# Attention heads in pairs: two heads share one PSUM accumulation, one product for the early keys of both, outputs taken out once per pair

## What is computed

```python
q = rope_tail(rms_norm(q, g_q_mla), cos, sin)      # MLA heads, 96 wide, values 64 wide
k = rope_tail(rms_norm(k, g_k_mla), cos, sin)
o_mla = blocked_causal_attention(pad_front(q), pad_front(k), pad_front(v_mla), MLA_QK ** -0.5)[:, PAD:]
...
o_fox = blocked_causal_attention(pad_front(qf), pad_front(kf), pad_front(vf), FOX_DIM ** -0.5, cum_log_f)[:, PAD:]
return jnp.concatenate([o_mla, o_fox], axis=-1) @ w_out
```

## Time and profile before

| | |
|---|---|
| median of 3 runs | 1344.78 us (1343.36 to 1344.78) |
| the profiled execution's own time | 1342.53 us |
| its span, first to last instruction | 1340.7 us |
| PE busy over the span | 1312.6 us (98%) |
| DVE, ACT, POOL busy | 969.4, 742.1, 362.3 us |
| granted PE clock, mean | 0.998 |

### The profile page before, as it was taken

How to read it: one execution, slowest core, us unless ns; L and a number is a source line. 1 busy time by engine, 2 the same in 40 slices (tenths; PEclk the granted TensorE clock), 3 DMA queues, 4 the chain that set the end, 5 groups by cost and what they waited for, 6 DMA issues and landing times. The chain is left out here.

```text
span 1340.7 us, 28848 instructions
## 1 busy us (share of the span) xinstructions
PE 1312.6 (98%) x10790; PEld 1289.3 (96%) x10790; DVE 969.4 (72%) x1462; ACT 742.1 (55%) x1198; POOL 362.3 (27%) x388
## 2 busy tenths in 40 slices
PE   9998999999999999999999999999999989999997
PEld 8887899999999999999999999999999989999997
DVE  6868877755487777555665669998559897999844
ACT  5456654444444554444546557666457986766642
POOL 4532133310011233100636214333102101433310
PEclk9999999999999999999999999999999999999999
DMA  9430245555554455555525545554554445555451
GB/s 314 161 114 1 82 172 188 188 192 186 184 182 167 157 198 185 208 180 177 208 103 187 191 158 201 183 184 159 189 212 164 175 165 189 194 186 185 159 194 55
DMA packets 35372, 230.53 MB, mean 172 GB/s; under 512 B 4062, under 2 KB 5214, under 8 KB 11910
## 3 DMA queue, kind: packets, MB, share of 16 engines
q1 hardware_dynamic: 34228, 226.99, 48.2%
q10 hardware_dynamic: 1058, 2.38, 0.5%
HBM read 228.17 MB, written 1.05 MB: 171 GB/s over the span
## 5 line engine op out<-in xcount | busy, mean ns | idle before, releaser
L382 DVE TENSOR_TENSOR wlo<-raw,whi 128x1024 fp32r<-128x1024 f32 (+1 forms) x446 | 526.1, 1182 | 89.7 <-ACT whi L376 87.6
L417 PE MATMUL ps<-xhi,whi 128*128 128x256 f32 (+2 forms) x2048 | 579.7, 283 | 3.8 <-DVE wlo L382 2.6
L418 PE MATMUL ps<-xlo,whi 128*128 128x256 f32 (+2 forms) x2048 | 577.9, 282 | 0.0
L419 PE MATMUL ps<-xhi,wlo 128*128 128x256 f32 (+2 forms) x2048 | 576.7, 282 | 0.0
L376 ACT ACTIVATE whi<-raw 128x1024 fp32r<-128x1024 f32 (+2 forms) x444 | 447.1, 1010 | 148.1 <-PE ps L419 138.4
L417 PEld LDWEIGHTS ps<-xhi,whi 128*128 128x128 f32 x2048 | 386.5, 189 | 8.8 <-issue 4.6
L419 PEld LDWEIGHTS ps<-xhi,wlo 128*128 128x128 f32 x2048 | 387.2, 189 | 0.0
L418 PEld LDWEIGHTS ps<-xlo,whi 128*128 128x128 f32 x2048 | 384.7, 188 | 0.3
L417 PE MATMUL ps<-hhi,whi 128*128 128x256 f32 (+1 forms) x1184 | 334.2, 282 | 4.5 <-DVE hlo L1706 3.6
L419 PE MATMUL ps<-hhi,wlo 128*128 128x256 f32 (+1 forms) x1184 | 333.2, 281 | 0.0
L418 PE MATMUL ps<-hlo,whi 128*128 128x256 f32 (+1 forms) x1184 | 333.0, 281 | 0.0
(11 more groups left out here) (303 smaller groups left out, 1274.6 us busy)
## 6 DMA issues: line engine op xcount, KB each, us to landing
raw<-w SPq DMA_DIRECT2D x182, 1024.0 KB, 4.8
raw<-w SPq DMA_DIRECT2D x40, 768.0 KB, 4.2
raw<-w SPq DMA_DIRECT2D x4, 512.0 KB, 5.3
h<-x_fm ACTq DMA_DIRECT2D x4, 272.0 KB, 5.6
out_fm<-h SPq DMA_DIRECT2D x8, 128.0 KB, 2.0
ws<-ws_src ACTq DMA_DIRECT2D x1, 512.0 KB, 3.6
bs<-bs_rows ACTq DMA_DIRECT2D x1, 512.0 KB, 5.0
consts<-constants SPq DMA_DIRECT2D x1, 508.0 KB, 10.3
```

The source lines that it names most:

```text
L382: nc.vector.tensor_tensor(wlo[:, w, 0:n], raw[:, slot, col:col + n], whi[:, w, 0:n].bitcast(F32), ALU.subtract).then_inc(wlo_done, 3 if fr ...
L417: nc.tensor.matmul(o, hi, xh, start=start, stop=False)
L418: nc.tensor.matmul(o, hi, xl, start=False, stop=False)
L419: mm = nc.tensor.matmul(o, lo, xh, start=False, stop=stop)
```

## The change

Two heads with neighbouring numbers (0 and 1, 2 and 3, ...) form a pair `k` and share one output bank (4 or 5, by `k`). The values are laid out anew: `v_main` holds for each pair three slots of 64 columns, the first head's values, zeros, the second head's values. A head's stationary operand is two neighbouring slots, so the other head's rows get zeros added, and both heads accumulate into all 128 rows of one bank. `v_early` holds the 16 early keys of the first head in rows 0 to 15 (columns 0 to 63) and those of the second in rows 32 to 47 (columns 64 to 127), and one product does both at the end of the second head's `values`. The first block's product now has 258 columns, since `prob_t` gets two zero columns ahead.

The narrow transposes of both heads are made in the `turn` of the second head (`second(j)`), into bank 6 always: first two that put the second head in rows 32 to 47, then two for the first head in rows 0 to 15. One ACT copy of 48 rows takes both to `prob_0`. `high` and `low` run once per pair, on all 128 rows. The probabilities get 4 buffers instead of 3, the d items a place of their own. d1 moves one place back in the list, to item 11, so its `turn` is at step 13. The constant `four` lies in a part of `extra`, and POOL clears two more small areas and one of 1024 columns. The copies of the 16 early keys' values by ACT are now two of 256 columns instead of one of 512, in each of the two attentions.

```diff
-        items = ([("d", 0)] + [("h", i) for i in range(HEADS)] + [("h", HEADS), ("d", 1)]
-                 + [("h", HEADS + i) for i in range(1, HEADS)])
+        items = ([("d", 0)] + [("h", i) for i in range(HEADS + 2)] + [("d", 1)]
+                 + [("h", HEADS + i) for i in range(2, HEADS)])
...
+        def second(j):
+            return items[j][0] == "h" and items[j][1] % 2 == 1
+        def early_turned(j):
+            return sum(items[x][0] == "d" or second(x) for x in range(j))
...
             def turn(j):
...
-                elif j <= LAST_SHARED:
-                    pe.wait_ge(pt0_done, j)
-                else:
-                    turn_bank = 6 + (j - LAST_SHARED) % 2
-                    pe.wait_ge(pt0_done, j - 1)
-                    pe.wait_ge(k_out, 2 * HEADS)
+                elif j < 6 or kind == "d" or second(j):
+                    pe.wait_ge(pt0_done, early_turned(j))
...
-                for x, a in enumerate((A, B)):
-                    nc.tensor.transpose(ps[0:META, turn_bank, x * P:(x + 1) * P], pr[:, a:a + META], ident)
+                if second(j):
+                    at = i % 4 * NPR
+                    for x, a in enumerate((A, B)):
+                        nc.tensor.transpose(ps[0:3 * META, 6, x * P:(x + 1) * P],
+                                            wide[:, at + a - 2 * META:at + a + META], ident)
+                    for x, a in enumerate((A, B)):
+                        nc.tensor.transpose(ps[0:META, 6, x * P:(x + 1) * P],
+                                            wide[:, at - NPR + a:at - NPR + a + META], ident)
...
             def values(i):
...
-                if i >= 2:
-                    pe.wait_ge(olo_done, i - 1)
+                if i >= 4 and o2 == 0:
+                    pe.wait_ge(olo_done, k - 1)
...
-                pe.wait_ge(d_done, i + 1)
-                nc.tensor.matmul(o, v_tok[:, w, 0, v], pt0, start=True, stop=False)
-                nc.tensor.matmul(o[:, HALO:T1], v_tok[:, w, 1, v], pt[:, 0:2 * P], start=False, stop=False)
-                nc.tensor.matmul(o[:, HALO + P:T1], v_tok[:, w, 2, v], pt[:, 2 * P:3 * P], start=False,
-                                 stop=True).then_inc(pv_done, 1)
+                nc.tensor.matmul(o, v[0], pt[:, 0:T1], start=o2 == 0, stop=False)
+                mm = nc.tensor.matmul(o[:, HALO + P:T1], v[1], pt[:, T1:T1 + P], start=False, stop=False)
+                if o2:
+                    pe.wait_ge(d_done, i + 1)
+                    mm = nc.tensor.matmul(o, v_early[:, w, hd // 2, :], pt0, start=False, stop=True)
+                mm.then_inc(pv_done, 1)
...
                     bank = 4 + k % 2 if w else 6 + kt % 2
-                    nc.scalar.activation(v_tok[0:n, w, kt, :], ps[0:n, bank, :], ACT.Copy).then_inc(vt_done, 1)
+                    if kt == 0:
+                        nc.scalar.activation(v_early[0:META, w, :, 0:P // 2], src[0:META, :, 0, :],
+                                             ACT.Copy).then_inc(s("v_early_done"), 1)
+                        nc.scalar.activation(v_early[2 * META:3 * META, w, :, P // 2:P], src[0:META, :, 1, :],
+                                             ACT.Copy).then_inc(vt_done, 1)
+                    else:
+                        nc.scalar.activation(v_main[:, w, kt - 1, :, 0:3:2, :], src, ACT.Copy).then_inc(vt_done, 1)
...
-                nc.scalar.activation(prob_0[i % 2][0:META, HALO:T1], ps[0:META, turn_bank, 0:2 * P],
-                                     ACT.Copy).then_inc(pt0_done, 1)
+                if second(j):
+                    nc.scalar.activation(prob_0[0:3 * META, i // 2 % 2, HALO:T1], ps[0:3 * META, 6, 0:2 * P],
+                                         ACT.Copy).then_inc(pt0_done, 1)
...
-                if st >= 4 and items[st - 4][0] == "h":
-                    if items[st - 4][1] >= HEADS:
-                        high(items[st - 4][1])
-                    low(items[st - 4][1])
+                if st >= 4 and second(st - 4):
+                    k = items[st - 4][1] // 2
+                    if 2 * k >= HEADS:
+                        high(k)
+                    low(k)
```

123 lines of the change are left out of this document (65 added, 58 removed).

## The result

The changed kernel took 1345.28 us, the median of 20 runs (1342.75 to 1352.32), against 1343.17 of the kernel before (20 runs, 1342.25 to 1345.13). The ratio is 1.0019, with a 95% interval of 1.0010 to 1.0027: 1.3 to 3.6 us slower, where 1.5 us of gain was forecast. That 1345.28 lies within the range on record, 1340.8 to 1345.4, is luck: the range counts from a median of three runs, 1344.78, which is 1.6 us above that of the twenty. The profiled execution has a span of 1343.5 us, against 1340.7.

A forecast was written before the change was run, and what follows sets the result against it. PE, busy 98% of the span, was taken to bound the kernel. Last values 1.6 us early, less 0.1 for value copies, gave 1.5 us gained: 1344.8 - 1.5 = 1343.3 us, range 1340.8 to 1345.4.

The forecast's parts named there:

- granted throughout: Whole kernel: PE is busy 98% of the span and has its full clock all the time.
- nothing beyond the lead: Step 9, PE's 1.42 us wait at 124.30: no gain credited there beyond the lead already won.
- Steps 4 to 8: DVE sets the pace and saves two `low`, 0.88 us: lead 0.9 us, 1.0 by step 12.
- so it can feed that pace: Steps 4 to 8: PE saves as much as DVE's 0.88 us, so it keeps up with DVE.
- The forecast wait of 0.9 us: Before d1's turn: PE waits about 0.9 us for ACT's copy of the early keys; lead down to 0.6.
- the 0.83 behind the halo: Behind d1: PE's existing 0.83 us wait goes away, since the early product now comes last.
- Step 14: DVE: the pair's `high` and `low` plus the split make the next maxima 0.2 us late; lead 0 at the last head's scores.
- The end: Last head: maxima start sooner, lead 0.9; last values no longer wait for `low`, starting at 150.8 us, 1.6 us early.
- The terms of single operations: Per operation: early product 0.44 us less a pair, wider transposes and `low` cost nothing more, value copies cost 0.1 us.
- PE's saving comes through whole: First rival, attention stretch: all of PE's 3.5 us comes off, 1341.3 us; 2.7 to 6.4 gained, chance 0.25.
- It does nothing: Rival: saved PE time becomes waiting as the softmax chain sets the pace; 1344.8 us or 0 to 0.7 less, chance 0.2.
- Slower through the turn of d1: Rival: PE and everything behind wait at d1's turn; 3.0 us of standing gives 1345.4 us, chance 0.05.

The follow-up runs named there:

- e3: Changed kernel with dead products (matmuls nobody reads) in four PE waits: key spread, values of heads 5 and 7, d1's turn; 1343.97 us, ratio 0.9991 to before.
- g2: Changed kernel with d1's turn in a bank of its own, so it no longer waits for ACT's copy; 1346.15 us, ratio 1.0023 to before.
- h1: g2 with ACT's copy of d1 made ahead of the weight split of step 12 instead of behind it; 1344.37 us, ratio 1.0006 to before.
- g1: Changed kernel with DVE's first late weight split after step 15 instead of step 14; 1344.92 us, ratio 1.0015 to before.
- i2: h2 with dead products at the key spread and before the values of heads 5 and 7; 1341.66 us, ratio 0.9991 to before.
- e2: Changed kernel with d1 back at item 10, its old place between heads 8 and 9; 1343.32 us, ratio 0.9986 to before.
- e4: Kernel before with the early product of even heads cut from 258 to 2 columns; 1344.98 us, ratio 1.0001 to before.
- e1: Changed kernel measured again without any edit; 1347.00 us, ratio 1.0022 to before.
- g4: Kernel before with dead products in its own PE waits; 1343.10 us, ratio 0.9991 to before.
- i1: Kernel before with the values of head 5 also waiting for head 6's large copy; 1351.76 us, ratio 1.0060 to before.
- h2: h1 with g1's later DVE split added; 1344.73 us, ratio 1.0009 to before.
- g3: e2 with dead products at the key spread and before the values of steps 9, 11, 14 and 18; 1340.72 us, ratio 0.9981 to before.

## Why the prediction was wrong

**The clock was not in the sum.** The prediction took from the earlier trace rows that PE has its full clock, "granted throughout", and that this would stay so. The trace of before shows otherwise at the very end, where PE has nothing to do:

```profile
1335.00:1340.70 5.70, 0.00 (x0) 0.00 (x0) 2.70 (x7) 0.00 (x0) 0.00 (x0) 0.50 0.54 184
```

It costed PE idle time at its own length, and credited "nothing beyond the lead" for the wait in step 9, without asking what a longer wait there brings. That wait went from 1.42 to 2.37 us, the one before the key spread from 0.65 to 1.00, and in 14 of 32 runs the clock was below 0.996, against 6 of 120 before. The one fall in the profile cost 1.57 us, and in the twenty runs the six at a clock of 0.998 have a median of 1343.5 us, all twenty 1345.3. This step failed first: it put at nothing what turned the small gain of the stretch (0.45 us in e3) into a loss. With the fall left out, no gain of 1.5 us is there either, and that is the work of the next steps.

**Steps 4 to 8, a lead of 0.9, then 1.0: mis-sized.** Without a fall (e3) the lead was 0.42 us at the scores of step 8 (19.30 against 19.72), 0.34 at the values of head 5 and -0.20 at those of head 7. The two `low` less on DVE are there. But that PE gives as much, "so it can feed that pace", failed: in step 6 DVE now waits for PE's scores (e3, full clock), where before no wait shows in steps 5 to 8:

```profile
113.06 0.65 DVE L1447 TENSOR_REDUCE soft<-ps 128x1 f32<-128x144 f32 x2 [0.41 <-PE ps L1128]
```

That wait takes back one of the two `low`. The next part goes on ACT, ahead of the values of head 5, where the copies of both halos now stand between the early keys' copy and the large one. From the one's start to the other's it is 0.36 us before and 0.70 in e3:

```profile
123.84 0.36 ACT L1830 ACTIVATE extra<-ps 16x256 f32<-16x256 f32 x1
124.11 0.19 ACT L1816 ACTIVATE extra<-extra 16x2 f32<-16x2 f32 x1
124.20 0.46 ACT L1839 ACTIVATE wide<-ps 128x384 f32<-128x384 f32 x1
...
123.53 0.37 ACT L1867 ACTIVATE extra<-ps 48x256 f32<-48x256 f32 x1
123.80 0.41 ACT L1853 ACTIVATE extra<-extra 16x2 f32<-16x2 f32 x2
124.23 0.49 ACT L1877 ACTIVATE extra<-ps 128x384 f32<-128x384 f32 x1
```

**d1: the turn right, the halo wrong.** The forecast wait of 0.9 us was 1.03, for the copy named (line 1852). But that the 0.83 behind the halo would go away, "as the early product comes last", failed. The wait was only hidden behind the one of the turn: when g2 took that away, 0.60 us of POOL came out, with the copy behind the split, 0.84 us in all (h1). The prediction looked in its last rival for a copy behind that split, and looked at the wrong copy: the 48-row copy is ahead of the split, that of d1 behind it.

**Step 14, 0.2 us late, lead 0 at the last head's scores: mis-sized.** The collision of `high`, `low` and split is there, and cost 1.0 us (g1), not 0.2. (The split was added at 1.2 us, where the earlier trace rows give 1.30, so the prediction's own rows make it 0.3 late.) DVE had to finish it before the maxima of step 15, on which the turn and the values of head 11 hang. At the scores of the last head the filled kernel is 1.1 us behind (46.10 against 45.00). Both pieces together make 1.74 us (i2 against e3). d1's place costs 2.8 (e2); the remaining 1.1 are not taken apart, and stay open.

**The end: right.** From 1.1 us behind at the last scores to 0.45 ahead at the output projection it is 1.55 us won; 1.6 were forecast. The last values wait for line 1862 and no longer for `low`, by 0.18 us. 

**The terms of single operations: right.** There are 16 passes of line 1181; the narrow transposes of 48 and of 16 rows take alike; `low` over 128 rows takes 0.42 us on average for all eight. The two value copies moved PE's wait for them from 0.33 to 0.51 us, where 0.1 was taken, and with what follows them 0.32 us are lost ahead of the first turn.

**The rivals.** "PE's saving comes through whole" falls by e3 and e4: 0.45 of 3.5 us came through without a fall, and 0.42 of e4's 1.7. The Trainium skill (Perfetto Trace Analysis, Identifying the Most-Contended Engine) was read too simply: it says to judge TensorE's headroom not by the busy share of the matmuls but by that of the weight loads. By that share PE (41.59 of 54.50 us, PEld in the earlier trace rows) is not the fullest engine here, DVE with 45.27 is. So the rule is no case for this rival, and the trace, in which most of PE's saved work became waiting, does not speak against it. "It does nothing" describes the changed kernel at an undisturbed clock: 0.45 us from the first turn on, 0.13 with the loss ahead of it. "Slower through the turn of d1" had the sign, and the place of part of the loss. But its point of decision, 2.4 us of standing there, was never reached.

**The signs.** The wait before d1's turn (1.03 us, where 0.7 to 1.2 were named) and the releaser of the last values came true. The maxima of step 8 stand 0.55 us earlier behind the first turn in e3 (20.78 against 21.33), not 0.9, and the output projection started at 156.08, not near 151.9.

The forecast sum, put right: 0.45 us won by the stretch at full clock (54.30 to 53.85), 0.32 lost ahead of it, and less 0.6 to 1.6 us for a fall in it. In 14 of 32 runs the clock was below 0.996, lower than in both profiled runs of the changed kernel, which hold one and two falls in the stretch.

## What to carry to other kernels

Where an edit takes work off the engine that runs at a gated clock, and the engine then stands longer, the granted clock belongs in the sum: look at what it does in the windows behind the two or three longest waits, and over several runs, since one profile may hold no fall. An experiment that is to take one saving alone should first be checked for how much it takes: e4 took half. Before crediting that a wait goes away, ask which wait ended just before it: taking off the last releaser shows the next. And an item that is moved by one place in a hand-written order should be followed through every engine's list at that step, small copies behind long ones first.

## What of the hardware was not expected

- Dead work in PE's waits makes a program faster: 3.0 us for the changed kernel (e3 against e1, same chip), and perhaps 1.0 for the kernel before (g4; its interval reaches to no difference).
- One added wait of 1.71 us, and nothing else, cost 7.8 us of median (i1, six runs; interval 1.0044 to 1.0075): 1.71 for itself and, by the low clocks, falls, of which the one in the profile took 1.4. Its runs of 1353 to 1355 us have clocks down to 0.990. Where their other falls lie no profile shows, since the profiled run was the one of 1347.13 us. g2 and h2 had one each in their profiles outside the attention, some 1010 us behind the first turn, 1.9 and 1.3 us after a wait of 1.47 us for DVE that the kernel before has too, without a fall behind it in its profile. So a wait of that length doesn't bring a fall each time. That part is open.

```profile
1107.62 0.36 PE L422 MATMUL ps<-hhi,whi 128*128 128x256 f32 x1 [1.47 <-DVE hlo L1723]
...
1109.50:1112.90 3.40, 3.14 (x15) 2.85 (x15) 1.66 (x4) 0.29 (x1) 0.00 (x0) 0.51 0.80 296
```

- Each fall of the granted clock before the last product lasted 3.4 us. (Every profile has one more at its end, 6.2 to 9.5 us at the lower level with PE idle.) What a fall costs depends on the waits behind it: 1.57 us of the stretch in the changed kernel's profile; in e1's, against e3, 0.6 for the first and 1.1 for the second, probably as waits behind them took up the rest.
- What brings the early fall, 6.1 to 6.5 us behind the first turn, in e1, g2, h1 and g3 was not found: from the first turn to there PE waits for the same 0.2 and 0.4 us in the kernels that have it and in those that don't. All four are paired kernels, 4 of 12 paired profiles against 0 of 4 of the others, so something besides the waits of theory A may bring falls. PE's longer wait for the copies of the values, 6 us ahead of the first turn, was not tested.
